# Two feed-forward down projections computed from seven products of halves instead of eight, in a fused three-block kernel on one Trainium2 core

## The chip, the cores and the metric

The kernel runs on one core of one Trainium2 chip. The metric is the device time of one execution in microseconds (us). A change is compared by running the kernel before and the changed one on the same chip.

## The reference

Two layers of a residual block, then a second block of another kind, on 512 tokens of width 1024 in float32. Each of the two layers is a mixer, a cross attention over 256 memory rows and a gated feed-forward, and each of the three is followed by a layer norm over a scaled residual. The change touches the feed-forward:

```
def conv_ffn(x, w_up, conv_w, conv_b, w_down):
    up = x @ w_up                         # 1024 -> 2 * 2816
    a, g = up[..., :D_FF], up[..., D_FF:]
    g = causal_dwconv(g, conv_w) + conv_b
    return (jax.nn.gelu(g) * a) @ w_down  # 2816 -> 1024
x = layer_norm(alpha * x + conv_ffn(...), ln_ffn_g[layer], ln_ffn_b[layer])
```

## The kernel before, in words

Every large product runs in three passes of float32r. An operand is split into a high half (ACT's copy to float32r) and a low half (the operand minus its high half, by DVE), and `mm3` adds high x high, high x low and low x high into one PSUM bank. A matmul has a 128x128 stationary operand and up to 512 moving columns.

Each engine has a program written out by hand; they meet on semaphores only. Weights come in chunks of 128x1024 values (256 rows by 512 columns). `load_to` (SP's queue) fills a ring of NR = 4 RAW buffers, `hi_to` (ACT) makes WH, `lo_to` (DVE) makes WL, both in rings of NH = 5. A chunk's RAW buffer is free when its low half is made; its WH and WL are free when PE has used them (`("used", i)`). So SP loads up to nine chunks ahead of PE, and ACT and DVE split up to five ahead.

The up projection of layer l is eleven column blocks `nb` of four chunks. A block yields two 128-row tiles of `a` and two of `g`, transposed (feature by token), in four PSUM banks. ACT copies g out (L1206), DVE convolves it (L1237 to L1242), ACT applies gelu (L1208), and DVE multiplies with `a` out of PSUM into `hT` (L1245), which holds 22 tiles of 128x512. In layer 1, DVE and SP also stream a vector product (`ada`, L1151 and L1155, with its loads) between the chunks. In layer 0 a value projection (`values_pe`) of the next cross attention stands between up and down.

The down projection (`down_pe`, `down_act`, `down_dve`) is two column halves j of 512. For each there are eleven chunks, with four token tiles t and two row tiles each: 22 x 4 x 3 = 264 matmuls of 512 columns a half, 528 a layer. The activation tile `hT[:, kt, :]` is split by `h_hi` (L1276) and `h_lo` (L1285) into eight slots of XH and XL (the first four of layer 1 into MH and ML). The last four chunks of the second half run token tile by token tile, so that the row norms (L690 to L677 on DVE, L682 and L684 on POOL) begin while PE still multiplies. After layer 0, the rows are transposed for the next stage; after layer 1, ACT squares and scales them (`square_act`, `xn_act`) for the second block.

POOL does little: row statistics (`norm_pool`), the loads of the gains (`load_gb`, L640 and L641) and a few loads for the second block (`early_pool`, L1379 to L1384).

## Time and profile before

| what | value |
|---|---|
| time, median of 3 runs | 1790.11 us (1788.22 to 1790.62) |
| span of the profiled execution | 1786.9 us |
| PE busy | 1761.0 us (99%) |
| DVE busy | 1012.8 us (57%) |
| ACT busy | 648.0 us (36%) |
| POOL busy | 99.3 us (6%) |
| HBM traffic | 181.58 MB read, 6.30 MB written, 105 GB/s |

The profiled execution gives a span and no time of its own beside it; the median of the runs is 3.2 us above that span. A matmul's record in the profile (some 370 to 390 ns) overlaps the next one's, so the number that counts is the distance between two starts.

### The profile page before, as it was taken

The numbers are of one execution on the slowest core, as the hardware profiler recorded it, in microseconds if no ns is written. First come the engines' busy times: TensorE is split into PE (matmuls) and PEld (weight loads), VectorE is DVE, ScalarE is ACT, GpSimd is POOL, SyncE is SP. The second block draws the span as 40 slices with busy tenths as digits, with TensorE's granted clock in tenths as the row PEclk, the third lists the DMA queues.
The fourth block names the chain that finished last, engine by engine and source line by source line (L and its number), as shares of the span: only waits on it lengthen the run. The fifth ranks groups of instructions, "written<-read, shape, count | busy, mean of one in ns | idle before, by whom it ended". The sixth has DMA issues, their size and how long they took to land.

```text
span 1786.9 us, 27394 instructions
## 1 busy us (share of the span) xinstructions
PE 1761.0 (99%) x11539; PEld 1464.1 (82%) x11539; DVE 1012.8 (57%) x1456; ACT 648.0 (36%) x1005; POOL 99.3 (6%) x136
## 2 busy tenths in 40 slices
PE   8999999999999999999999999999999999999998
PEld 7888978988888889888997888888888767777766
DVE  5477256444445555454724755566555585566784
ACT  5232352332234433223234233332433653344552
POOL 3102001000000001000200200000001100011000
PEclk9999999999999999999999999999999999999999
DMA  9323312533333323333331264444331422112512
GB/s 298 114 94 113 112 32 82 158 95 95 96 104 107 94 83 119 112 100 108 117 107 49 75 218 154 142 153 130 125 97 45 151 60 72 38 38 62 176 36 83
DMA packets 146010, 189.67 MB, mean 106 GB/s; under 512 B 7800, under 2 KB 95092, under 8 KB 145120
## 3 DMA queue, kind: packets, MB, share of 16 engines
q1 hardware_dynamic: 140928, 172.59, 31.3%
q0 software_dynamic: 3488, 10.07, 1.8%
q10 hardware_dynamic: 1472, 5.26, 0.8%
q8 instruction: 92, 1.51, 0.4%
q14 instruction: 30, 0.25, 0.0%
HBM read 181.58 MB, written 6.30 MB: 105 GB/s over the span
## 4 chain that ended last, share of the span: by engine, by line
PE 93%; DVE 4%; issue 1%; ACT 1%; POOL 1%; DMA 0%; SPq 0%; DVEq 0%; ACTq 0%
PE ps L326 27%; PE ps L328 27%; PE ps L327 27%; PE ps L965 2%; PE ps L989 2%; PE ps L515 1%; PE ps L2186 1%; PE ps L2206 1%; PE ps L1592 1%; PE ps L2200 1%; PE ps L2220 0%; DVE LATE L2267 0%; PE ps L2323 0%; DVE WL L310 0%; DMA BIG<-mem 0%
## 5 line engine op out<-in xcount | busy, mean ns | idle before, releaser
L310 DVE TENSOR_TENSOR WL<-RAW,WH 128x1024 fp32r<-128x1024 f32 x289 | 350.4, 1222 | 499.6 <-ACT WH L300 498.5
L326 PE MATMUL ps<-XH,WH 128*128 128x512 f32 (+1 forms) x1416 | 523.9, 370 | 3.9 <-DVE XL L1462 2.1
L300 ACT ACTIVATE WH<-RAW 128x1024 fp32r<-128x1024 f32 x289 | 303.4, 1058 | 595.2 <-PE ps L328 569.1
L328 PE MATMUL ps<-XH,WL 128*128 128x512 f32 (+1 forms) x1416 | 517.6, 366 | 0.0
L327 PE MATMUL ps<-XL,WH 128*128 128x512 f32 (+1 forms) x1416 | 517.3, 365 | 0.0
L326 PE MATMUL ps<-WH,XH 128*128 128x512 f32 x784 | 313.5, 400 | 2.4 <-DVE WL L310 1.1
L326 PEld LDWEIGHTS ps<-XH,WH 128*128 128x128 f32 x1416 | 267.1, 189 | 51.7 <-issue 6.6
L328 PE MATMUL ps<-WH,XL 128*128 128x512 f32 x784 | 305.8, 390 | 0.0
L327 PE MATMUL ps<-WL,XH 128*128 128x512 f32 x784 | 305.4, 390 | 0.0
L328 PEld LDWEIGHTS ps<-XH,WL 128*128 128x128 f32 x1416 | 267.1, 189 | 43.5
L327 PEld LDWEIGHTS ps<-XL,WH 128*128 128x128 f32 x1416 | 267.2, 189 | 40.7
L326 PEld LDWEIGHTS ps<-WH,XH 128*128 128x128 f32 x784 | 147.2, 188 | 36.5 <-issue 5.1
L328 PEld LDWEIGHTS ps<-WH,XL 128*128 128x128 f32 x784 | 147.1, 188 | 31.4
L327 PEld LDWEIGHTS ps<-WL,XH 128*128 128x128 f32 x784 | 147.3, 188 | 29.4 <-issue 1.2
L682 POOL TENSOR_SCALAR SM<-SM 128x1 f32<-128x1 f32 x28 | 34.3, 1226 | 1014.0 <-DVE SM L668 1013.7
L1208 ACT ACTIVATE SCR<-SCR,VEC 128x512 f32<-128x512 f32 x44 | 31.8, 724 | 112.6 <-DVE SCR L1242 112.6
L522 ACT ACTIVATE XH<-ps 128x512 fp32r<-128x512 f32 x48 | 25.8, 597 | 107.1 <-PE ps L515 107.0
L1285 DVE TENSOR_TENSOR XL<-BIG,XH 128x512 fp32r<-128x512 f32 x84 | 53.7, 684 | 1.4 <-ACT XH L1276 1.4
L1245 DVE TENSOR_TENSOR BIG<-SCR,ps 128x512 f32<-128x512 f32 x44 | 30.2, 687 | 34.8 <-ACT SCR L1208 34.8
L1276 ACT ACTIVATE XH<-BIG 128x512 fp32r<-128x512 f32 x84 | 47.4, 616 | 2.3 <-PE ps L328 2.3
L326 PE MATMUL ps<-WH,MH 128*128 128x256 f32 (+1 forms) x144 | 42.6, 296 | 0.0
L327 PE MATMUL ps<-WL,MH 128*128 128x256 f32 (+1 forms) x144 | 42.4, 295 | 0.0
(349 smaller groups left out, 1757.3 us busy)
## 6 DMA issues: line engine op xcount, KB each, us to landing
RAW<-ffn_w_up SPq DMA_DIRECT2D x176, 256.0 KB, 3.3
RAW<-ffn_w_down SPq DMA_DIRECT2D x44, 512.0 KB, 3.6
RAW<-w_in SPq DMA_DIRECT2D x33, 512.0 KB, 4.0
RAW<-xa_wkv SPq DMA_DIRECT2D x32, 512.0 KB, 3.9
RAW<-c_w_in SPq DMA_DIRECT2D x24, 512.0 KB, 3.8
LATE<-w_ada SPq DMA_DIRECT2D x24, 512.0 KB, 5.1
RAW<-xa_wq SPq DMA_DIRECT2D x16, 512.0 KB, 5.7
RAW<-xa_wo SPq DMA_DIRECT2D x16, 512.0 KB, 3.7
```

What stands on the lines that cost most here:

```text
L300: e.activation(halves_of(i)[0][:, :, 0:w], raw(i)[:, :, 0:w], ACT.Copy).then_inc(*w_hi.up(i))
L310: e.tensor_tensor(wl[:, :, 0:w], raw(i)[:, :, 0:w], wh[:, :, 0:w].bitcast(F), ALU.subtract).then_inc(*w_lo.up(i))
L326: e.matmul(o, lh, rh, start=start, stop=False)
L327: e.matmul(o, lh, rl, start=False, stop=False)
L328: return e.matmul(o, ll, rh, start=False, stop=stop)
L682: e.tensor_scalar(vr[:, t:t + 1], mv[:, t, 1:2], 1e-5, None, ALU.add).then_inc(*ln_g.up((n, t, "eps")))
L965: r = e.matmul(b[:, 256 * (t % 2):256 * (t % 2) + 256], qT[:, 2 * h + k, 128 * t:128 * t + 128], KT[:, 2 * h + k, :], start=k == 0, stop=k ...
L989: r = e.matmul(b[:, :], VT[:, mt, 256 * h + 128 * d:256 * h + 128 * d + 128], PT[h % 2][:, mt, :], start=mt == 0, stop=mt == 1)
L1208: e.activation(gc[i], gc[i], ACT.Gelu_apprx_tanh, bias=vec(f"fcb{l}", j)).then_inc(*ffn_a.up(("gelu", l, j)))
L1245: e.tensor_tensor(hT[:, j, :], c, ps.tile((("up", l, nb), i))[:, :], ALU.mult).then_inc(*ps.empties((("up", l, nb), i), ffn_v, ("h", l, j)))
L1276: e.activation(h_home(l, j, kt)[0], hT[:, kt, :], ACT.Copy).then_inc(*x_hi.up(("h", l, j, kt)))
L1285: e.tensor_tensor(lo, hT[:, kt, :], hi.bitcast(F), ALU.subtract).then_inc(*x_lo.up(("h", l, j, kt)))
```

## The change

With the activations A (512 x 2816) and the weights B (2816 x 1024) both cut in two along both sides, B11 = rows 0 to 1407 and columns 0 to 511, and so on. Token tiles t are 0 and 1 in the upper half of A, 2 and 3 in the lower one. The four blocks of the output come from

```
S1 = A21 + A22   S2 = S1 - A11   S3 = A11 - A21   S4 = A12 - S2
T1 = B12 - B11   T2 = B22 - T1   T3 = B22 - B12   T4 = B21 - T2
P1 = A11 B11   P2 = A12 B21   P3 = S4 B22   P4 = A22 T4
P5 = S1 T1     P6 = S2 T2     P7 = S3 T3
C11 = P1+P2   C12 = P1+P6+P5+P3   C21 = P1+P6+P7+P4   C22 = P1+P6+P7+P5
```

- **Products.** Seven of 256 x 1408 x 512, each two token tiles by eleven row tiles by three passes: 66 matmuls, 462 a layer. A chunk is now 128 rows of two weight halves (a: B11 and T1; b: T2 and T3; c: B21 and B22) or two row tiles of T4 (e), 39 chunks a layer for 22; each serves 12 matmuls instead of 24 (6 for the last).
- **Weight sums.** `sums_pool` makes T1 to T4 on POOL in the up projection, in 22 steps a layer (row tile k, column half h): two loads of 256 KB with 1 KB pieces, four `tensor_tensor` of 128x256, and one store of 512 KB to HBM (`weight_sums`). Two tiles alternate; the load of step j+1 is issued behind the store of step j and waits for the store of step j-1. SP's loads of the chunks a, b and e wait for the store of their k.
- **Activation sums and items.** `down_pool` makes S1 to S4 by four `tensor_tensor` of 128x256 for each k. The operands of the products are 40 items a layer of 128x512, in order: pairs A (A11 and S1), pairs B (S3 and S2), then C (A12) and D (S4) by turns, then E (A22). ACT makes each item's high half (`item_hi`, L1368 of the changed kernel); DVE makes the low half of A, C and E, and POOL that of B and D (`item_lo_pool`, L1382). Eight slots of XH and XL, as before, with MH and ML for the first four items of layer 1.
- **Order at the end of up.** In layer 1 `item_hi` of items 0 and 1 stands ahead of column block 9, and waits for the last stores of the sums; the two that stood at blocks 4 and 7 are gone. `up_act` and `up_dve` take gelu, convolution and items by turns in block 10.
- **Assembly.** After P1 and P5 (step 20) and P6 and P7 (step 21), ACT copies P1 to SBUF (U), DVE runs twelve operations of 128x512 on U and the rows, and POOL later adds U to six row halves. P2 and P3 end together, then P4 runs by token tile; rows 0 and 1 need P2 and P3, rows 2 and 3 need P4. `early_pool` now stands behind `down_pool`.

```diff
+    FAST = [(name, q + i) for q in range(0, 11, 2) for name in "ab" for i in range(min(2, 11 - q))]
+    FAST += [("c", k) for k in range(11)] + [("e", q) for q in range(6)]
+    def pair(q):
+        return min(2, 11 - 2 * q)
+    def w_fast(l):
+        first["ffn", l] = len(chunks)
+        w = I["ffn_w_down"][l]
+        for name, k in FAST:
+            if name == "a":
+                chunks.append(([((0, 1), 512, w[128 * k:128 * k + 128, 0:512].unsqueeze(1)),
+                                ((1, 2), 512, d_sum[l][k][:, 1:2, :])], 512, (l, k)))
+            if name == "b":
+                chunks.append(([((0, 1), 512, d_sum[l][k][:, 0:1, :]), ((1, 2), 512, d_sum[l][k][:, 3:4, :])], 512, (l, k)))
+            if name == "c":
+                chunks.append(([((0, 2), 512, w[1408 + 128 * k:1536 + 128 * k, :].rearrange("p (k n) -> p k n", k=2))],
+                               512, None))
+            if name == "e":
+                v = d_sum[l][2 * k:2 * k + pair(k)]
+                chunks.append(([((0, pair(k)), 512, v[:, :, 2, :].rearrange("k p n -> p k n"))], 512, (l, 2 * k + pair(k) - 1)))
...
+            if chunks[i][2] is not None:
+                for h in range(2):
+                    e.wait_ge(*sum_out[h].at(chunks[i][2]))
...
+        for nb in range(10):
+            if (l, nb) == (1, 9):
+                item_hi(e, 1, 0)
+                item_hi(e, 1, 1)
             hi_to(e, first["up", l, nb] + 4 + NH)
...
+        hi_to(e, first["up", l, 10] + 3 + NH)
+        for i in range(2):
+            gate_act(e, l, 10, i)
+            item_hi(e, l, i if l == 0 else 2 + i)
+        hi_to(e, first["up", l, 10] + 4 + NH)
+        gelu_act(e, l, 10, 0)
+        if l == 0:
+            item_hi(e, 0, 2)
+        gelu_act(e, l, 10, 1)
+        if l == 0:
+            item_hi(e, 0, 3)
...
+    def item_hi(e, l, n):
+        name, k = ITEMS[n]
+        if l and n < 4:
+            for h in range(2):
+                e.wait_ge(*sum_out[h].at((1, 10)))
+        elif n < 8 + 4 * l:
+            e.wait_ge(*gemm.at((("up", l, 10), 3)))
+        else:
+            e.wait_ge(*gemm.at(("used", first["ffn", l] + item_last(n - 8))))
+        if name in "AB":
+            e.wait_ge(*dn_g.at(("s", l, k)))
+        elif name == "D":
+            e.wait_ge(*dn_g.at(("s4", l, 2 * k + pair(k) - 1)))
+        else:
+            e.wait_ge(*ffn_v.at(("h", l, 10 + 2 * k + pair(k))))
+        e.activation(item_view(n, item_home(l, n)[0]), item_from(n), ACT.Copy).then_inc(*x_hi.up(("item", l, n)))
...
+    def item_lo_pool(e, l, n):
+        e.wait_ge(*x_hi.at(("item", l, n)))
+        hi, lo = item_home(l, n)
+        e.tensor_tensor(item_view(n, lo), item_from(n), item_view(n, hi).bitcast(F), ALU.subtract).then_inc(
+            *x_lo_g.up(("item", l, n)))
...
+    def sum_load(e, l, j):
+        k, h = j // 2, j % 2
+        if k:
+            e.wait_ge(*sum_out[h].at((l, k - 1)))
+        else:
+            e.wait_ge(*(gemm.at(("kvv", 1, 3, 1)) if l else xa_pe.at(("pv", 0, 3, 1))))
+        w = I["ffn_w_down"][l].rearrange("(i r) (j n) -> r i j n", i=2, j=2)
+        to = sum_tile(l, h).rearrange("p (i j n) -> p i j n", i=2, j=2)
+        for i in range(2):
+            e.dma_start(to[:, i, :, :], w[128 * k:128 * k + 128, i, :, 256 * h:256 * h + 256]).then_inc(*sum_in[h].up((l, k)))
+    def sums_pool(e, l):
+        sum_load(e, l, 0)
+        sum_load(e, l, 1)
+        for j in range(22):
+            k, h = j // 2, j % 2
+            x = sum_tile(l, h)
+            b11, b12, b21, b22 = [x[:, 256 * i:256 * i + 256] for i in range(4)]
+            e.wait_ge(*sum_in[h].at((l, k)))
+            e.tensor_tensor(b22, b22, b12, ALU.subtract).then_inc(*sum_g.up(("t3", l, j)))
+            e.tensor_tensor(b12, b12, b11, ALU.subtract).then_inc(*sum_g.up(("t1", l, j)))
+            e.wait_ge(*sum_g.at(("t3", l, j)))
+            e.tensor_tensor(b11, b11, b22, ALU.add).then_inc(*sum_g.up(("t2", l, j)))
+            e.wait_ge(*sum_g.at(("t2", l, j)))
+            e.tensor_tensor(b21, b21, b11, ALU.subtract).then_inc(*sum_g.up(("t4", l, j)))
+            e.wait_ge(*sum_g.at(("t4", l, j)))
+            e.dma_start(d_sum[l][k][:, :, 256 * h:256 * h + 256], x.rearrange("p (i n) -> p i n", i=4)).then_inc(
+                *sum_out[h].up((l, k)))
+            if 1 <= j < 21:
+                sum_load(e, l, j + 1)
+    def down_pool(e, l):
+        if l == 0:
+            e.wait_ge(*rel_out.at("rel"))
+        def rest(k):
+            n = ITEMS.index(("B", k))
+            item_lo_pool(e, l, n)
+            e.wait_ge(*(x_lo.at(("item", l, ITEMS.index(("A", k))))))
+            e.tensor_tensor(hT[:, k, 0:256], hT[:, 11 + k, 0:256], ring[k % 2][:, 256:512], ALU.subtract).then_inc(
+                *dn_g.up(("s4", l, k)))
+        for k in range(11):
+            a11, a21, a22 = hT[:, k, 0:256], hT[:, k, 256:512], hT[:, 11 + k, 256:512]
+            s3, s2 = ring[k % 2][:, 0:256], ring[k % 2][:, 256:512]
+            e.wait_ge(*ffn_v.at(("h", l, 11 + k)))
+            if k >= 2:
+                e.wait_ge(*dn_g.at(("s4", l, k - 2)))
+            e.tensor_tensor(s3, a11, a21, ALU.subtract).then_inc(*dn_g.up(("s3", l, k)))
+            e.wait_ge(*dn_g.at(("s3", l, k)))
+            e.tensor_tensor(a21, a21, a22, ALU.add).then_inc(*dn_g.up(("s1", l, k)))
+            e.wait_ge(*dn_g.at(("s1", l, k)))
+            e.tensor_tensor(s2, a21, a11, ALU.subtract).then_inc(*dn_g.up(("s", l, k)))
+            if k:
+                rest(k - 1)
+        rest(10)
+        for q in range(3):
+            item_lo_pool(e, l, 23 + 2 * q)
+        for u in range(2):
+            e.wait_ge(*ln_v.at((("ffn", l), "sum", u)))
+            for name, t, j in (("x12", u, 1), ("x21", 2 + u, 0), ("x22", 2 + u, 1)):
+                x = XR[:, t, 512 * j:512 * j + 512]
+                e.wait_ge(*ln_v.at((("ffn", l), "p7" if name == "x22" else name, u)))
+                e.tensor_tensor(x, x, U[u], ALU.add).then_inc(*dn_g.up((name, l, u)))
+        for q in range(3, 6):
+            item_lo_pool(e, l, 23 + 2 * q)
...
+        for s, (name, k) in enumerate(ITEMS[0:22]):
+            e.wait_ge(*w_lo.at(i0 + s))
+            ready(s)
+            of = ((1, 0), (5, 256)) if name == "A" else ((6, 256), (7, 0))
+            for half, (p, at) in enumerate(of):
...
+                if name == "ffn":
+                    sums_pool(e, l)
+                    down_pool(e, l)
```

In these rows of program order, names are those of the diff: LAST is POOL's pair of sum tiles, `weight_sums` the sums in HBM, BIG holds `hT`. First POOL in layer 1, from the load of the gains on, before:

```order
L640 DMA GB<-ln_ffn_g 128x1024
L641 DMA GB<-ln_ffn_b 128x1024
L1379 DMA LAST<-w_2 64x512
L1380 DMA LAST<-a_2 64x512
L1382 DMA LAST<-rel_padded 128x8x256
L1384 DMA SCR<-cstd 128x128
```

and in the changed kernel, from behind the same two loads on:

```order
L1398 DMA LAST<-ffn_w_down 128x2x256 x4
L1409 TENSOR_TENSOR LAST<-LAST 128x256
L1410 TENSOR_TENSOR LAST<-LAST 128x256
L1412 TENSOR_TENSOR LAST<-LAST 128x256
L1414 TENSOR_TENSOR LAST<-LAST 128x256
L1416 DMA weight_sums<-LAST 512x1x256
L1409 TENSOR_TENSOR LAST<-LAST 128x256
L1410 TENSOR_TENSOR LAST<-LAST 128x256
L1412 TENSOR_TENSOR LAST<-LAST 128x256
L1414 TENSOR_TENSOR LAST<-LAST 128x256
L1416 DMA weight_sums<-LAST 512x1x256
L1398 DMA LAST<-ffn_w_down 128x2x256 x2
```

The loads that stood right behind the gains come after 22 such steps and the whole of `down_pool`. Next POOL at the start of the first changed down projection (L1437 to L1441 are S3, S1 and S2, L1382 the low half of a B item, L1429 is S4):

```order
L1437 TENSOR_TENSOR BIG<-BIG 128x256
L1439 TENSOR_TENSOR BIG<-BIG 128x256
L1441 TENSOR_TENSOR BIG<-BIG 128x256
L1382 TENSOR_TENSOR XL<-BIG,XH 128x512
L1429 TENSOR_TENSOR BIG<-BIG 128x256
L1437 TENSOR_TENSOR BIG<-BIG 128x256
L1439 TENSOR_TENSOR BIG<-BIG 128x256
L1441 TENSOR_TENSOR BIG<-BIG 128x256
```

The last five of these rows are what POOL repeats for each k; before, POOL had nothing in this place. Last, ACT in layer 1 in the changed kernel (L1254 copies g out, L1259 is gelu, L327 the weights' high halves, L1368 an item's), from the end of column block 8:

```order
L1254 ACTIVATE SCR<-ps 128x512
L1259 ACTIVATE SCR<-SCR,VEC 128x512
L1368 ACTIVATE MH<-BIG 128x512 x2
L327 ACTIVATE WH<-RAW 128x1024 x4
L1254 ACTIVATE SCR<-ps 128x512
L1259 ACTIVATE SCR<-SCR,VEC 128x512
L1254 ACTIVATE SCR<-ps 128x512
L1259 ACTIVATE SCR<-SCR,VEC 128x512
L327 ACTIVATE WH<-RAW 128x1024 x3
L1254 ACTIVATE SCR<-ps 128x512
```

The two items stand ahead of all of ACT's work for block 9; before, the row L300 x4 followed gelu at once.

## Rows read from the trace of the kernel before

**Rows 1.** The page: busy time of each engine, and PE's clock in slices.

```profile
PE 1761.0 (99%) x11539; PEld 1464.1 (82%) x11539; DVE 1012.8 (57%) x1456; ACT 648.0 (36%) x1005; POOL 99.3 (6%) x136
...
PEclk9999999999999999999999999999999999999999
```

**Rows 2.** Windows, second down projection, PE (span, busy, count, clock, DMA, GB/s).

```profile
1265.30:1384.90 119.60, 119.60 (x529) 1.00 0.28 87
```

**Rows 3.** Timeline of DVE, first down projection (start us, us, what, [idle before]).

```profile
603.05 1.23 DVE L310 TENSOR_TENSOR WL<-RAW,WH 128x1024 fp32r<-128x1024 f32 x1 [3.01 <-ACT WH L300]
604.19 1.28 DVE L1285 TENSOR_TENSOR XL<-BIG,XH 128x512 fp32r<-128x512 f32 x2
```

**Rows 4.** Timeline of ACT, same place and columns.

```profile
601.96 1.06 ACT L300 ACTIVATE WH<-RAW 128x1024 fp32r<-128x1024 f32 x1 [3.34 <-PE ps L328]
602.92 1.14 ACT L1276 ACTIVATE XH<-BIG 128x512 fp32r<-128x512 f32 x2
```

**Rows 5.** Windows of the two up projections, all engines (busy us, count).

```profile
313.00:552.00 239.00, 239.00 (x1143) 201.63 (x1142) 110.51 (x133) 72.37 (x88) 0.43 (x1) 1.00 0.36 108
1026.00:1265.00 239.00, 239.00 (x1142) 201.31 (x1142) 141.33 (x188) 73.04 (x90) 0.38 (x1) 1.00 0.50 157
```

**Rows 6.** The page: DMA issues of the whole run.

```profile
RAW<-ffn_w_up SPq DMA_DIRECT2D x176, 256.0 KB, 3.3
RAW<-ffn_w_down SPq DMA_DIRECT2D x44, 512.0 KB, 3.6
```

**Rows 7.** POOL, grouped by line and form (xcount | busy us, mean ns | idle before).

```profile
L1550 POOL TENSOR_TENSOR LAST<-LAST,SM 128x512 f32<-128x512 f32 x4 | 4.0, 1040 | 13.1 <-DVE SM L1534 13.1
...
L1373 POOL TENSOR_SCALAR SM<-SM 128x1 f32<-128x1 f32 x4 | 0.8, 190 | 10.7 <-ACT SCR L1365 10.7
```

**Rows 8.** Timeline of POOL at a row norm of the last down projection.

```profile
1370.56 1.31 POOL L682 TENSOR_SCALAR SM<-SM 128x1 f32<-128x1 f32 x1 [91.43 <-DVE SM L668]
...
1375.19 0.19 POOL L1373 TENSOR_SCALAR SM<-SM 128x1 f32<-128x1 f32 x1 [2.67 <-ACT SCR L1365]
```

**Rows 9.** Timeline of DVE at the same place.

```profile
1370.51 1.28 DVE L671 SCALAR_TENSOR_TENSOR XR<-XR,SM,GB 128x1024 f32<-128x1024 f32 x1
```

**Rows 10.** Timeline of POOL before the first up projection's gains are loaded.

```profile
309.20 1.40 POOL L684 TENSOR_TENSOR SM<-SM 128x1 f32<-128x1 f32 x1
...
312.91 0.53 POOL L641 DMA_DIRECT2D GB<-ln_ffn_b  x1
```

**Rows 11.** Timeline of DVE at the same place.

```profile
308.95 1.22 DVE L310 TENSOR_TENSOR WL<-RAW,WH 128x1024 fp32r<-128x1024 f32 x1
```

**Rows 12.** DMA issues from 1020 to 1040 us (KB each, us to landing).

```profile
GB<-ln_ffn_g POOLq DMA_DIRECT2D x1, 512.0 KB, 4.2
GB<-ln_ffn_b POOLq DMA_DIRECT2D x1, 512.0 KB, 5.9
```

**Rows 13.** DMA issues, whole run, the largest load on POOL's queue.

```profile
LAST<-rel_padded POOLq DMA_DIRECT2D x1, 1024.0 KB, 7.4
```

**Rows 14.** Timeline of POOL where the second up projection's gains are loaded.

```profile
1025.85 0.53 POOL L641 DMA_DIRECT2D GB<-ln_ffn_b  x1
```

**Rows 15.** Timeline of ACT in the last two column blocks of the second up projection.

```profile
1220.10 1.06 ACT L300 ACTIVATE WH<-RAW 128x1024 fp32r<-128x1024 f32 x1 [4.38 <-PE ps L328]
...
1228.51 1.04 ACT L300 ACTIVATE WH<-RAW 128x1024 fp32r<-128x1024 f32 x1
...
1242.81 1.06 ACT L300 ACTIVATE WH<-RAW 128x1024 fp32r<-128x1024 f32 x1 [4.38 <-PE ps L328]
```

**Rows 16.** Timeline of ACT at the end of the first up projection.

```profile
552.64 1.06 ACT L300 ACTIVATE WH<-RAW 128x1024 fp32r<-128x1024 f32 x1 [4.38 <-PE ps L328]
```

**Rows 17.** Timeline of DVE, the last row norm of the second down projection.

```profile
1385.13 0.69 DVE L690 SCALAR_TENSOR_TENSOR XR<-XR,ps 128x512 f32<-128x512 f32 x1 [0.34 <-PE ps L328]
```

More of the change, by code:

```diff
@@ L1278, in h_lo @@
[L1278 to L1292 removed]
+            if (l, nb) == (1, 9):
+                item_lo(e, 1, 0)
+                item_lo(e, 1, 1)
@@ new lines, in up_dve @@
+            for c in range(4 if nb else 0):
+                if l:
+                    side()
+                lo_to(e, first["up", l, nb] + min(c + 1, 3 if nb == 10 else 4) + NH)
+                if l:
+                    side()
+            if nb < 10:
+                lo_to(e, first["up", l, nb] + 4 + NH)
+                for i in range(2):
+                    conv_dve(e, l, nb, i)
+                    gated_dve(e, l, nb, i)
+        conv_dve(e, l, 10, 0)
+        if l == 0:
+            item_lo(e, 0, 0)
@@ L1297, in behind @@
                 turn_pe(e, n, t)
-        if l == 0:
-            values_pe(e, 1, 0)
-        for j in range(2):
-            gemm_n(e, (*n, j), lambda kt, t, j=j: h_x(l, j, kt, t), 11, final=behind if j else None, ready=lambda kt, j=j: x_lo.at(("h", l, j, kt)))
+        for u in range(2):
+            ps.take(("down", l, 4, u))
+            for w in ps.vacant(("down", l, 4, u)):
+                e.wait_ge(*w)
+        for q in range(2):
+            for u in range(2):
+                last(q, u)
@@ L1303, in down_act @@
+        for u in range(2):
+            for q in range(2, 6):
+                last(q, u)
+                if (u, q) in ((0, 5), (1, 3)):
+                    behind(u)
+        ps.back(*[("down", l, 4, u) for u in range(2)])
     def down_act(e, l):
-        n = ("ffn", l)
+        n, i0 = ("ffn", l), first["ffn", l]
+        limit = n_in2 if l else n_chunks
+        item_hi(e, l, 4)
         if l == 0:
             values_act(e, 1, 0)
-        for c in range(11):
-            hi_to(e, first[(*n, 0)] + c + 1 + NH)
-            h_hi(e, l, 0, c + 3)
```

371 lines of the change are left out of this document (250 added, 121 removed).

## Prediction

> **What bounds the kernel now.** The page comes first: PE is busy for 99% of the span, and its granted clock is the higher of its two levels (2.4 GHz) in every slice, while DVE, ACT and POOL have room [rows 1]. So the down projections cost what PE's matmuls cost, and the window over the second one shows it: PE is busy in all of its 119.60 us, with 529 matmuls started, which is 0.2265 us each [rows 2]. Inside it DVE works 2.4 us and ACT 2.1 us for each chunk of 5.44 us [rows 3, 4]. Nothing in this stage is waited for but PE. The two up projections are as full [rows 5], so all that the change adds there lies beside PE, if it keeps its due times.
>
> **What is removed.** 66 matmuls a layer, 132 in all: 132 x 0.2265 = 29.9 us from the path of PE. The form of the matmuls and their operands' sizes are the same, so I take the same distance between starts.
>
> **What is added on ACT and DVE.** A chunk or an item now serves 12 matmuls, 2.72 us. DVE needs 1.14 us for a weight low half (the distance of its start to the next) and 0.64 for an item [rows 3], so for a pair k of an A and a B item (5.44 us of PE) 2 x 1.14 + 0.64 = 2.9 us. ACT needs 2 x 1.06 + 2 x 0.57 = 3.3 us [rows 4]. Both fit; cost nothing while PE is the cover. A chunk every 2.72 us asks 193 GB/s of SP's queue. Loads of 512 KB land 3.6 us after their issue, and those in two pieces of 256 KB after 3.3 each [rows 6]; a RAW buffer comes round every 4 x 2.72 = 10.9 us and needs about 3.7 + 1.1 + 1.2 = 6 of them. No cost.
>
> **POOL in the down projection.** Here the cover is thinnest. A POOL `tensor_tensor` of 128x512 took 1.04 us, a 128x1 operation 0.19 [rows 7]; I put 128x256 between them, at 0.62. For each k POOL runs four of these and one of 512: 3.5 us, some 4.0 with gaps of 0.09. Alone it would keep up with 5.44. But a POOL operation waits for DVE: the 128x1 operation that takes 0.19 us where DVE is not at work took 1.31 where DVE had just begun 1.28 us on two SBUF operands [rows 8, 9], and a second one 1.40 where the next DVE operation of that kind ran [rows 10, 11]. All of DVE's weight and item low halves have two SBUF operands. If the two engines excluded each other in full, a k would take 3.5 + 2.9 = 6.4 us; if POOL fills DVE's pauses well, 5.44 or less. The waits of the trace are all of POOL for DVE, and part of POOL's time (the 0.19) moves no data, so I take 6.0. The due times: item A3 is needed 5 x 2.72 = 13.6 us after A0, and POOL makes its two k by 2 x 6.0 = 12.0, ACT and DVE add 1.2, which leaves 0.4. From A3 to A9 PE takes 12 items, 32.6 us, and POOL six k, 36.0. That is 3.4 - 0.4 = 3.0 us of waiting a layer, 6.0 for both. At 5.44 it is nothing, at 6.4 it is 6.2 a layer, 12.4 for both; these are the ends.
>
> The Trainium skill (SBUF — State Buffer, Who interferes with whom) says that a DVE instruction with two SBUF inputs and a GpSimd instruction that reads SBUF exclude each other, whichever began first. The trace agrees for POOL behind DVE, at 1.31 us for 0.19; no row shows DVE behind POOL. By that rule the sum would have the 12.4 us in place of 6.0.
>
> **The weight sums in the up projection.** One step is four additions, a store and, behind it, the two loads of the next step, whose landing it then waits for. The additions take 4 x 0.62 + 0.3 = 2.8 us alone; DVE is busy for 59% of the second up projection [rows 5] and can hold each of them up by 0.35, which gives 4.2; I take 3.4. The DMA part: two loads of 512 KB on POOL's queue, issued 0.62 us apart, landed 4.2 and 5.9 us after their own issues [rows 12], so the second ended 2.3 us behind the first, and what is fixed is 1.9. A load of 1024 KB with 1 KB pieces took 7.4 [rows 13]. If the store and the loads share the queue one behind the other, landing is 1.9 + 2.3 + 2.3 = 6.5 us after the store's issue; if they run side by side, 1.5 of issuing, 1.9 and 1.2 make 4.6. I take the middle, 5.6. Of the 22 steps 20 wait so: 22 x 3.4 + 20 x 5.6 + 1.6 for two bare stores = 188 us, between 155 and 224.
>
> The room in layer 1: the last load of the gains is issued at 1025.85 [rows 14], lands 5.9 later, and the first sums' rows some 2.3 after that, at 1034. ACT now stands at item 0 of block 9, where before it split weights at 1228.51; it has the high half of block 10's first chunk since 1220.10, and block 10 begins at 1242.8, when the chunk before it is used [rows 15]. So PE runs until 1242.8 + 5.4 = 1248.2, and ACT must be back by 1246.0. From the last store's issue to there go S of k 0 and 1 and the item, 5.7 us. That leaves 1240.3 - 1034 = 206 us. 188 fits, 224 is 18 us late. In layer 0 nothing is needed before PE has left up (552.6 [rows 16]) and the value projection behind it (5.5 us more): from 312.91 [rows 10] + 8.2 to 553.7 are 232 us, which holds even 224. So this costs nothing at what I take, 18 us at its upper end. What is covered here has no cover beyond 18 us of slack; that is the step with the largest error.
>
> **The ends of the stage.** P3 takes the banks of P5, due 4.1 and 4.8 us after item 20 ends; DVE frees them after six operations of 0.65, at 3.9, if ACT's copies are there: 0.3 us a layer, from 0 to 2. Rows 0 and 1 now start together, when P2 and P3 are done, and DVE needs about 7.5 us each (with four adds and statistics of 0.7, two passes of 1.28, POOL's 0.85 and a weight of 1.14); PE comes to the transposes of row 1 after 24 + 21 + 12 matmuls and the first transposes, at 13.8: 1.0 us in layer 0. Row 3 of layer 1 used to begin 0.2 us behind PE's last matmul [rows 17], with its rows 5.44 us apart and 0.34 of it idle; P4's tiles come 4.76 apart: 0.35 us. `early_pool` moves behind `down_pool`, which ends when item 33 is split, about 35 us before the stage's end; its largest load takes 7.4 us [rows 13]: nothing.
>
> **Sum.** -29.9 + 6.0 + 0.6 + 1.0 + 0.35 = -22 us. It is made against the span of 1786.9, which the median of the runs exceeds by 3.2; taken off the median of 1790.1 it gives **1768 us**.
>
> **Rivals.**
> - *All hidden.* POOL slips between DVE's operations. For it: DVE waits 3.0 us in each chunk [rows 3], and POOL alone needs 4.0 of 5.44. Against it: the waits of [rows 8 to 11]. Only the 2 us at the ends stay: 1790.1 - 29.9 + 2 = 1762, from 1759 to 1764.
> - *DVE and POOL exclude each other in full*, the 6.4 us a k: 1790.1 - 29.9 + 12.4 + 2 = 1775, up to 1779 if the burst of twelve DVE operations comes on top. This is the rule named above. For it: POOL's waits; against it: no DVE operation in the trace is longer for POOL's sake.
> - *The sums come late in layer 1 only*, by up to 18 us: PE stands still in block 10 for just as long: 1774 to 1786. For it: up is also where DMA is busiest, 157 GB/s without the sums in layer 1 [rows 5].
> - *The sums come late in both layers*, and the kernel is slower than before. It decides from 24 us of lateness on, which is 230 us for the 22 steps. If the sums' DMAs take 7.5 us a step beside the other streams, the steps take 22 x 4.2 + 20 x 7.5 + 1.6 = 244 us, 38 late in layer 1 and 12 in layer 0, and 9 from the rest: 1790.1 - 29.9 + 59 = 1819. Against it: the load that was longest for its size took 7.4 us for twice the loads' bytes.
> - *The gain isn't made*: the matmuls go but start further apart, because two of the halves and the weights change every 12 matmuls. Nothing in the window of [rows 2] depends on the chunk, so this has little: about 1790.
>
> **Chances.** The forecast's own case (1764 to 1774) has 0.45, all hidden 0.23, full exclusion 0.12, late in layer 1 0.11, late in both 0.06, no gain 0.03. A measurement of this kernel tells 0.2%, 3.6 us, from no change. Faster by more: the first four, less a little of the late case, 0.90; within it 0.04; slower 0.06. The range 1759 to 1785 leaves out the last two cases, the end of the late one and a tail below.
>
> **What would show it.** In the profile of the changed kernel: 132 matmuls fewer, still 0.2265 us apart; in the A and B part of both down projections pauses of PE behind POOL's item low halves, 2 to 4 us in each; POOL operations of 128x256 between 0.6 and 1.9 us, the long ones beside DVE; a sum step of some 9 us; the last store of the sums in layer 1 before 1240 and no pause of PE in block 10. Wrong would be: a pause of PE of more than 3 us in block 10 of layer 1 (the sums), DVE operations stretched beyond 1.3 us (exclusion both ways), or a PE pause at P3's or P4's first matmul (banks).

## The result

The changed kernel took 1856.1 us, the median of four runs (1854.62 to 1859.96), against 1790.4 us before: a ratio of 1.0374, with a 95% interval from 1.0362 to 1.0387. It is 3.7% slower; the prediction was faster by 1.2%. The profiled execution spans 1854.8 us.

From the page of the changed kernel: busy time of each engine, the granted clock in 40 slices, the chain that ended last, and the three groups of DMAs that are new.

```profile
PE 1756.0 (95%) x11407; PEld 1451.7 (78%) x11407; DVE 1110.9 (60%) x1468; ACT 677.9 (37%) x1035; POOL 528.8 (29%) x578
...
PEclk9999999999999999999999999996999899999999
...
PE 50%; POOL 20%; DMA 13%; DVE 11%; issue 4%; ACT 2%; SPq 0%; ACTq 0%; DVEq 0%; POOLq 0%
...
RAW<-weight_sums SPq DMA_DIRECT2D x68, 256.0 KB, 3.6
...
LATE<-ffn_w_down POOLq DMA_DIRECT2D x44, 256.0 KB, 4.6
weight_sums<-LATE POOLq DMA_DIRECT2D x22, 512.0 KB, 3.4
```

The 132 matmuls are gone (11539 in [rows 1]), but PE's busy time fell by only 5 us, and it is now 99 us short of the span, where it was 26 short. The clock falls in two slices, and 44% of the chain that ended last is POOL, DMA and DVE, where before they had 5% of it.

The time splits at the starts of five matmuls that both kernels have: the first of each down projection, the first 128x512 one of the stage behind the first down projection, the first one behind the last product of the second down projection (it makes a bias tile), and the first product of the second block. In us, each with what it would be if only the matmuls had gone:

| stretch | before | bare gain | changed |
|---|---|---|---|
| down projection of layer 0 and the rows' turn behind it | 152.8 | 137.8 | 167.8 |
| from there to the down projection of layer 1, up projection included | 554.4 | 554.4 | 587.4 |
| down projection of layer 1 | 119.7 | 104.7 | 133.4 |
| from the end of its products to the second block's first | 11.5 | 11.5 | 17.0 |
| all the rest | 948.6 | 948.6 | 949.3 |

So 30.0, 33.0, 28.6 and 5.5 us were lost at four places. The two down projections lose for the same reasons, the stretch between them for another. First the largest single pause: PE stood still in block 10 of layer 1's up projection. These are PE's own rows at the places of its longest pauses (start us, us, engine, line, operation, and in brackets the idle time before it with its releaser). Where the text counts pauses, it takes the distance of two starts less 0.2265 us, which is some 0.15 more than the idle time in brackets:

```profile
570.64 0.80 PE L359 MATMUL ps<-WH,XH 128*128 128x512 f32 x1 [5.02 <-DVE WL L337]
...
638.95 0.77 PE L359 MATMUL ps<-WH,XH 128*128 128x512 f32 x1 [4.83 <-DVE XR L1581]
...
1290.61 0.80 PE L359 MATMUL ps<-XH,WH 128*128 128x512 f32 x1 [29.63 <-DVE SM L1195]
...
1394.41 0.77 PE L359 MATMUL ps<-WH,XH 128*128 128x512 f32 x1 [4.71 <-DVE XR L1581]
...
1438.55 0.50 PE L359 MATMUL ps<-WH,XH 128*128 128x512 f32 x1 [3.66 <-DVE WL L337]
```

The releaser of the 29.6 us is a small DVE operation of the side work, which is only the last link. ACT's own rows at that time show the first:

```profile
1285.24 0.63 ACT L1368 ACTIVATE MH<-BIG 128x512 fp32r<-128x512 f32 x1 [42.45 <-DMA weight_sums<-LAST]
1287.65 0.63 ACT L1368 ACTIVATE MH<-BIG 128x512 fp32r<-128x512 f32 x1 [1.79 <-POOL BIG L1441]
1288.19 3.88 ACT L327 ACTIVATE WH<-RAW 128x1024 fp32r<-128x1024 f32 x4
```

ACT stood 42.5 us at item 0 of the second down projection, whose home is `MH`, until the last store of the weight sums had landed. Four high halves of weights were queued behind it, DVE had nothing to split, and PE ran dry. POOL's rows of the last steps of those sums show how long one takes:

```profile
1272.84 0.75 POOL L1416 DMA_DIRECT2D weight_sums<-LAST  x1 [0.30 <-POOL LAST L1414]
1273.51 1.42 POOL L1398 DMA_DIRECT2D LAST<-ffn_w_down  x2
1278.63 0.71 POOL L1409 TENSOR_TENSOR LAST<-LAST 128x256 f32<-128x256 f32 x1 [3.70 <-DMA LAST<-ffn_w_down]
1279.32 0.71 POOL L1410 TENSOR_TENSOR LAST<-LAST 128x256 f32<-128x256 f32 x1
1280.00 0.71 POOL L1412 TENSOR_TENSOR LAST<-LAST 128x256 f32<-128x256 f32 x1
1280.79 0.72 POOL L1414 TENSOR_TENSOR LAST<-LAST 128x256 f32<-128x256 f32 x1
1281.81 0.75 POOL L1416 DMA_DIRECT2D weight_sums<-LAST  x1 [0.30 <-POOL LAST L1414]
```

This step, with DVE idle, took 9.0 us. Over all of layer 1 the first addition began at 1049.8 and the last store at 1281.8: 232 us, 11.0 a step; in layer 0 it was 322.0 to 546.3, 10.7 a step. The waits of the whole run, grouped by who waits for whom (us in total, times, longest), say how much of it is the loads:

```profile
POOL LAST L1409 <- DMA LAST<-ffn_w_down: 103.5, 21, 7.6
...
POOL LATE L1409 <- DMA LATE<-ffn_w_down: 93.6, 21, 6.6
ACT XH L1368 <- POOL BIG L1441: 72.8, 18, 4.6
...
PE ps L359 <- DVE WL L337: 28.9, 16, 5.0
```

The loads are 4.9 us of waiting a step in layer 1 (103.5 / 21), and 2.1 of issuing lie ahead of them.

The first and the third line of the table are the down projections. There POOL's rows over two k of the A and B part of layer 1 read:

```profile
1339.67 1.80 POOL L1382 TENSOR_TENSOR XL<-BIG,XH 128x512 fp32r<-128x512 f32 x1 [2.27 <-ACT XH L1368]
1341.43 1.71 POOL L1429 TENSOR_TENSOR BIG<-BIG 128x256 f32<-128x256 f32 x1
1343.29 1.53 POOL L1437 TENSOR_TENSOR BIG<-BIG 128x256 f32<-128x256 f32 x1
1344.89 0.74 POOL L1439 TENSOR_TENSOR BIG<-BIG 128x256 f32<-128x256 f32 x1
1345.71 0.74 POOL L1441 TENSOR_TENSOR BIG<-BIG 128x256 f32<-128x256 f32 x1
1346.41 1.30 POOL L1382 TENSOR_TENSOR XL<-BIG,XH 128x512 fp32r<-128x512 f32 x1
...
1354.44 1.80 POOL L1382 TENSOR_TENSOR XL<-BIG,XH 128x512 fp32r<-128x512 f32 x1 [2.27 <-ACT XH L1368]
```

and DVE's in the same stretch:

```profile
1340.57 3.66 DVE L337 TENSOR_TENSOR WL<-RAW,WH 128x1024 fp32r<-128x1024 f32 x2 [0.24 <-ACT WH L327]
1347.21 1.04 DVE L1376 TENSOR_TENSOR XL<-BIG,XH 128x512 fp32r<-128x512 f32 x1 [2.99 <-ACT XH L1368]
1348.18 1.76 DVE L337 TENSOR_TENSOR WL<-RAW,WH 128x1024 fp32r<-128x1024 f32 x1
1352.93 0.69 DVE L1376 TENSOR_TENSOR XL<-BIG,XH 128x512 fp32r<-128x512 f32 x1 [2.99 <-ACT XH L1368]
1353.87 1.23 DVE L337 TENSOR_TENSOR WL<-RAW,WH 128x1024 fp32r<-128x1024 f32 x1 [0.25 <-ACT WH L327]
```

POOL's sums take 0.74 us alone and 1.53 or 1.71 beside DVE, its low half 1.30 or 1.80; and DVE's weight low half takes 1.23 alone, as in [rows 3], but 1.76 or more beside POOL. POOL comes round in 14.77 us for two k, 7.4 a k against PE's 5.44: 6.25 of work, stretched, and 1.1 of waiting for ACT, which splits the second of two A items and a weight before the B item that POOL waits for. PE paused eight times in this part of layer 1, for 12.7 us together. Last, the windows over the pauses (busy us of each engine, granted clock as a share of 2.4 GHz, DMA share, GB/s):

```profile
570.00:575.00 5.00, 4.36 (x10) 3.48 (x11) 5.00 (x4) 2.47 (x4) 4.70 (x4) 0.50 0.55 160
...
1262.00:1290.00 28.00, 0.00 (x0) 0.00 (x0) 2.48 (x3) 2.98 (x4) 16.48 (x23) 0.57 0.29 94
1290.00:1295.00 5.00, 4.39 (x10) 3.48 (x11) 4.90 (x8) 2.56 (x4) 0.00 (x0) 0.50 0.63 173
1295.00:1300.00 5.00, 5.00 (x20) 4.07 (x19) 4.14 (x7) 1.21 (x2) 0.00 (x0) 0.84 0.75 242
```

After the pause of 5.0 us and after the one of 29.6 PE worked at 0.50, the lower level (1.2 GHz): 10 matmuls in 4.4 us, where at 0.2265 us each it would be 19. So a pause costs more than its own length: 33.0 us for the one of 29.8.

### The profile page after: what moved, and what is told of

The parts are those of the page before. It is cut to its first block, busy times and chain, and to the rows that moved or that the text cites. A ratio compares the mean times of both kernels' runs of the same rounds, so it can differ in the third digit from the quotient of the medians.

```text
span 1854.8 us, 27838 instructions
## 1 busy us (share of the span) xinstructions
PE 1756.0 (95%) x11407; PEld 1451.7 (78%) x11407; DVE 1110.9 (60%) x1468; ACT 677.9 (37%) x1035; POOL 528.8 (29%) x578
## 4 chain that ended last, share of the span: by engine, by line
PE 50%; POOL 20%; DMA 13%; DVE 11%; issue 4%; ACT 2%; SPq 0%; ACTq 0%; DVEq 0%; POOLq 0%
PE ps L359 14%; PE ps L360 13%; PE ps L361 13%; DMA LAST<-ffn_w_down 6%; DMA LATE<-ffn_w_down 6%; DVE WL L337 3%; POOL weight_sums L1416 2%; POOL BIG L1437 2%; PE ps L1001 1%; PE ps L1025 1%; POOL LATE L1409 1%; POOL BIG L1429 1%; POOL XL L1382 1%; POOL LAST L1414 1%; POOL LATE L1410 1%
## 5 line engine op out<-in xcount | busy, mean ns | idle before, releaser
L337 DVE TENSOR_TENSOR WL<-RAW,WH 128x1024 fp32r<-128x1024 f32 x323 | 425.3, 1331 | 382.3 <-ACT WH L327 381.1
L359 PE MATMUL ps<-XH,WH 128*128 128x512 f32 (+1 forms) x1416 | 526.9, 372 | 36.1 <-DVE SM L1195 29.6
L327 ACT ACTIVATE WH<-RAW 128x1024 fp32r<-128x1024 f32 x323 | 338.1, 1056 | 504.5 <-PE ps L361 452.8
L359 PE MATMUL ps<-WH,XH 128*128 128x512 f32 x740 | 303.3, 410 | 37.8 <-DVE WL L337 27.4
L361 PE MATMUL ps<-WH,XL 128*128 128x512 f32 x740 | 292.8, 396 | 0.0
L360 PE MATMUL ps<-WL,XH 128*128 128x512 f32 x740 | 292.4, 395 | 0.0
L361 PEld LDWEIGHTS ps<-WH,XL 128*128 128x128 f32 x740 | 141.2, 191 | 31.1
L1259 ACT ACTIVATE SCR<-SCR,VEC 128x512 f32<-128x512 f32 x44 | 31.9, 724 | 127.6 <-DVE SCR L1303 127.6
L1368 ACT ACTIVATE XH<-BIG 128x512 fp32r<-128x512 f32 (+1 forms) x76 | 45.5, 602 | 73.6 <-POOL BIG L1441 72.8
L1376 DVE TENSOR_TENSOR XL<-BIG,XH 128x512 fp32r<-128x512 f32 (+1 forms) x44 | 38.8, 882 | 49.2 <-ACT XH L1368 49.2
L1382 POOL TENSOR_TENSOR XL<-BIG,XH 128x512 fp32r<-128x512 f32 (+1 forms) x32 | 52.0, 1630 | 28.8 <-ACT XH L1368 28.7
L1409 POOL TENSOR_TENSOR LATE<-LATE 128x256 f32<-128x256 f32 x22 | 27.2, 1235 | 93.6 <-DMA LATE<-ffn_w_down 93.6
```

Source lines behind the costliest of these rows:

```text
L327: e.activation(halves_of(i)[0][:, :, 0:w], raw(i)[:, :, 0:w], ACT.Copy).then_inc(*w_hi.up(i))
L337: e.tensor_tensor(wl[:, :, 0:w], raw(i)[:, :, 0:w], wh[:, :, 0:w].bitcast(F), ALU.subtract).then_inc(*w_lo.up(i))
L359: e.matmul(o, lh, rh, start=start, stop=False)
L360: e.matmul(o, lh, rl, start=False, stop=False)
L361: return e.matmul(o, ll, rh, start=False, stop=stop)
L1368: e.activation(item_view(n, item_home(l, n)[0]), item_from(n), ACT.Copy).then_inc(*x_hi.up(("item", l, n)))
```

## The experiments

The theory that came out of these rows has **two causes**: the sums of weights come late (33 us), and POOL and DVE hold one another up in the down projections (most of 58 us). The rival for each was that the loss would stay when its alleged cause went: that the added DMA traffic or the added work itself is what costs. What a later run changes is told against the changed kernel unless it says otherwise.

**1. The loads earlier.** In each step the next step's two loads are issued behind the third addition, not behind the store.

```
+            if 1 <= j < 21:
+                sum_load(e, l, j + 1)      # behind t2, ahead of the fourth addition
...
-            if 1 <= j < 21:
-                sum_load(e, l, j + 1)      # behind the store
```

> The loads of the next sums step are issued behind the third addition instead of behind the store. Theory (the sums are late because each step waits for a load that is issued last): a step falls from 10.5 us to about 8.2, the last store of layer 1 is issued near 1230 us instead of 1281.8, and the 29.8 us pause of PE in column block 10 of layer 1 is gone, with the low clock behind it: 33 us less, about 1822 us. The pauses inside both down projections stay (20 and 21 us). Rival (the step is bound by the DMA engines, which also carry weights and the ada stream): a step of 10 us or more, and a pause still above 20 us, 1845 us or more.

It took 1821.5 us (1.0172 of before, 1.0143 to 1.0202), 34.6 less. The step of layer 1 fell to 9.5 us, where 8.2 were hoped for, as POOL now waits for the store before it can load into the tile behind it:

```profile
1235.76 1.72 POOL L1412 TENSOR_TENSOR LAST<-LAST 128x256 f32<-128x256 f32 x1
1238.69 1.45 POOL L1398 DMA_DIRECT2D LAST<-ffn_w_down  x2 [1.21 <-DMA weight_sums<-LAST]
1240.16 0.75 POOL L1416 TENSOR_TENSOR LAST<-LAST 128x256 f32<-128x256 f32 x1
1241.20 0.75 POOL L1418 DMA_DIRECT2D weight_sums<-LAST  x1 [0.30 <-POOL LAST L1416]
```

But the last store went out at 1247.2 in place of 1281.8, and that is enough: the pause in block 10 is gone, the stretch between the down projections takes 554.4 us, that of before, and no other stretch changed by more than 1.1. The same bytes move in both, so it was not their amount that cost the 33 us but when the last of them landed.

**2. The items of layer 1 later.** The high and low halves of items 0 to 3 of layer 1 stand where layer 0 has them, in block 10, so that ACT and DVE split block 10's weights before they wait for item 0.

```
-            if (l, nb) == (1, 9):
-                item_hi(e, 1, 0)
-                item_hi(e, 1, 1)
...
-            item_hi(e, l, i if l == 0 else 2 + i)
+            item_hi(e, l, i)
```

> The sums are untouched; only the high and low halves of items 0 to 3 of layer 1 are moved from the top of column block 9 to behind the copies of block 10, as in layer 0. Theory (PE stands still because ACT is parked at item 0 with all its weight work behind it, not because PE needs the item): ACT goes on, the last store still comes near 1282 us, PE ends block 10 near 1280 and waits for the first item until about 1288; the pause falls from 29.8 us to 6 to 10, total about 1833 us. Rival (the sums' lateness is paid in full wherever the wait stands): no change, 1855 us.

It took 1836.8 us (a single run), 19.3 less. PE runs block 10 and stops at the first item instead:

```profile
1291.78 0.77 PE L359 MATMUL ps<-WH,MH 128*128 128x512 f32 x1 [13.78 <-issue]
```

So 30 us of pause became 14, and the stretch between the down projections lost 13.9 us in place of 33.0: less than half of the price was the lateness itself, the rest was what the program order had put behind the wait. The pause came out 4 to 8 us longer than expected; the last store was issued at 1286.5 in this run, not near 1282.

**3. DVE's part of the collision smaller.** The low halves of the weights in the a and b chunks are made for half their columns only; the other half of `WL` keeps old values, so this run leaves that part of the correction out.

```
+            if any(first["ffn", l] <= i < first["ffn", l] + 22 for l in range(2)):
+                w = 256
```

> DVE makes the low halves of the A and B chunks for 256 of each 512 columns only; the rest of WL keeps old values. So DVE's two-operand work for a k falls from 2.9 us to about 1.8, and POOL's is untouched. Theory (DVE and POOL exclude each other, so that a k costs the sum of their times, 7.38 us now): about 6.2 us a k, PE's pauses in the A and B part fall from 12 to about 5 us a layer, the bank pause of 5 us at P3 too, total about 1836 us. Rival (POOL is too slow by itself, or its chain of waits is): POOL's period stays 7.38 us a k, total 1853 to 1856.

It took 1832.0 us (a single run), 24.1 less. POOL's item low halves begin 12.74 us apart for two k, 6.4 a k in place of 7.4, with the wait for ACT still in it:

```profile
1324.13 1.29 POOL L1384 TENSOR_TENSOR XL<-BIG,XH 128x512 fp32r<-128x512 f32 x1 [2.27 <-ACT XH L1370]
...
1336.86 1.29 POOL L1384 TENSOR_TENSOR XL<-BIG,XH 128x512 fp32r<-128x512 f32 x1 [2.27 <-ACT XH L1370]
```

Nothing of POOL's own work was taken away. A shorter DVE operation made POOL faster, which is the collision and not POOL's load.

**4. POOL's part smaller.** The four sums of a k are made for 16 of 256 columns from k = 2 on (the rest keep old values).

```
+            m = 256 if k < 2 else 16
+            a11, a21, a22 = hT[:, k, 0:m], hT[:, k, 256:256 + m], hT[:, 11 + k, 256:256 + m]
```

> POOL's S1 to S4 are made for 16 columns of 256 (from k = 2 on), so most of the activation sums are left out; all waits and the order stay. Theory (the time of POOL's additions beside DVE makes the pauses): POOL needs some 2.5 us a k, the pauses of the A and B part (12 and 13 us) and the 5 us at P3's bank in each layer go to 0 to 2 us, total about 1822 us; the pause in block 10 of layer 1 stays. Rival (the chain item B behind item A through ACT and POOL binds, 2.27 us of waiting in each two k): pauses of at least 5 us a layer stay, total 1840 us or more.

It took 1813.0 us (a single run), 43.1 less. Of the pauses in the A and B parts one of 1.3 us is left, and the ones at P3's bank fell from about 5 us to 0 and 1.1: they were DVE's lateness, carried on. The two down stretches took 146.3 and 114.9 us. This is what the down projections cost if the sums of hidden rows were nearly free, and layer 1 is still 10 us above its bare 104.7; 5.2 of them are the pause at the last e chunk, 1.1 the one at P3's bank.

**5. The same work on DVE.** S1 to S4 and the low halves of the B and D items (not of weights, as the expectation has it) move to DVE, POOL keeps the additions of U. The sums of weights stay as the change has them.

```
-    on_pool = ("B", "D")
+    on_pool = ()
...
+            rest_dve(e, l, s + 7)          # S4 of this k, S3, S1, S2 of k + 2
```

> All of S1 to S4 and the low halves of the B and D weights move from POOL to DVE; POOL keeps only the additions of U at the down projection's end. The weight sums in the up projection stay as in the change. Theory 'POOL and DVE hold each other up in the down projection': without POOL there, DVE has 4.9 us of work a k at its undisturbed durations (L337 at 1.22, two items' low halves, four sums of about 0.35 each) against 5.44 us of PE, so the pauses of 1.3 to 2.3 us in the A/B part and most of the 5 us at P3's bank go in both layers, about 34 us with the clock behind them as in the run with narrow sums; the pause of about 29 us in block 10 of layer 1 stays: about 1,820 us. Rival 'what takes the time is the work itself, wherever it runs': DVE becomes the engine that is waited for, pauses of 0.5 to 1.5 us stay at each k, and the time is 1,835 us or more.

It took 1822.7 us (a single run), 33.4 less, with 122 operations more on DVE and as many fewer on POOL. In the down projections one of these sums takes 0.42 or 0.43 us there against 0.73 to 1.72 on POOL. The down stretches are 152.7 and 115.8 us. That DVE itself becomes the bound is true only at the start of each stage (5.1 us in layer 0, and 1.2 and 0.8 in layer 1), where five items come at once. At the end, the pause of 4.9 us at layer 1's last e chunk is still there.

**6. Both.** Runs 1 and 5 together.

> Both edits together: the loads of the next step's two blocks issued behind the third of the step's four additions instead of behind its store, and the sums of the down projection on DVE. Theory 'two separate causes, one in each projection': the first alone gave 1,821.5 us (34.6 below the change), the second should give about as much, and since they act at different places they add up: 1,785 to 1,790 us, the time of the kernel before, with the pauses at P3's bank, at the last e chunk and in the tail left. Rival 'the two hide one another' (the late sums also set the start of the down items): 1,800 us or more.

It took 1787.4 us (1785.8 to 1791.9, eight runs; 0.9990 of before, 0.9979 to 1.0001). The two gains, 34.6 and 33.4, made 68.7 together, so the causes are separate, and with them undone the change costs nothing. Nor does it gain anything clear of noise: 29.9 us of matmuls are gone and the time is that of before. From its page:

```profile
PE 1741.0 (98%) x11407; PEld 1444.5 (81%) x11407; DVE 1147.5 (64%) x1590; ACT 679.1 (38%) x1035; POOL 376.4 (21%) x456
...
PE 83%; DVE 12%; issue 2%; DMA 1%; ACT 1%; POOL 1%; SPq 0%; DVEq 0%; ACTq 0%
```

Layer 0's stretch is 149.6 and layer 1's 116.6, each 3 us better than before and not 15; the one behind layer 1 is 16.5 where 11.5 was. At P3's bank no pause is left in either layer. The rest of the study asked where these 29 us are.

**7. The order at the stage's end, first try.** To run 6: the last e chunk's low half inside row 0's work, and P5 taken out of its bank before the two x11 rows.

```
             row(t)
+            if t < 1:
+                lo_to(e, min(i0 + 34 + NH, limit))
```

> As the run with both edits, and two changes of order on DVE: the low half of the last e chunk's weight item stands in front of the second row instead of behind the first row's whole work, and the evacuation of P5 stands ahead of the two x11 rows, so that the bank for P3 comes free earlier. Theory: each of the pauses of 3.8 to 4.9 us at these places was DVE's order and nothing else, so 3 to 4 of them (both layers) go and the time falls by 6 to 12 us against the run with both edits alone: 1,775 to 1,782 us, below the kernel before. Rival 'the pauses at the end are the latency of P3's own chain': the pause only moves to the next bank, and the time is within 2 us of the run with both edits alone.

It took 1787.6 us (0.9988 of before, 0.9977 to 1.0000): no gain. In layer 1 the pause of 4.95 us at the last e chunk became one of 2.7 there and one of 2.8 at the transposes behind it. The time is the rival's, but its reason is not shown: P3's bank had cost nothing in run 6, so that half of the edit had nothing to gain.

**8. The rows in another order.** To run 6: the last e chunk's low half ahead of row 0, row 1's first addition between row 0's norm and its end, POOL's square root of the next row ahead of the RMS scale.

```
+        lo_to(e, min(i0 + 34 + NH, limit))
+        first_half(0); second_half(0); norm(0)
+        first_half(1); row_end(0); second_half(1); norm(1)
```

> As the run with both edits (1,787.4 us), and the rows' work on DVE at the down projections' end put in another order: the low half of the last e chunk stands ahead of row 0 instead of behind it, row 1's first addition and statistics stand between row 0's norm and its end (where DVE waited 0.83 to 0.85 us for POOL's square root), and in layer 1 POOL makes the next row's square root before the row's own RMS scale. Theory 'these pauses are DVE's order': the pause of 4.95 us before the last e chunk in layer 1 goes with the 2 to 3 us of half clock behind it, the tail of layer 1 shortens from 13.1 us by about 4, in layer 0 the pauses of 0.9 and 1.9 us go: 10 to 14 us less, 1,773 to 1,778 us, under the kernel before. Rival 'the earlier work only moves the pause', as when the low half was put inside row 0 and P5's evacuation first (1,787.6): 1,784 us or more.

It took 1787.2 us (0.9989 of before, 0.9980 to 0.9999). Layer 1's down projection fell from 116.6 to 109.1 us, as expected, and the stretch behind it rose from 16.5 to 23.5, where the theory had it fall; the whole lies in the rival's range. ACT's rows there show why: row 3 left DVE at 1383.7, but its square stands at 1387.07, behind row 2's scale, bias copies and a weight.

```profile
1384.11 1.15 ACT L1694 ACTIVATE BIG<-XR,SM 128x1024 f32<-128x1024 f32 x1 [1.87 <-POOL SM L1700]
1385.17 1.06 ACT L1760 ACTIVATE VH<-ps 128x512 f32<-128x512 f32 x2
1386.12 1.06 ACT L328 ACTIVATE WH<-RAW 128x1024 fp32r<-128x1024 f32 x1
1387.07 1.05 ACT L1690 ACTIVATE SCR<-XR 128x1024 f32<-128x1024 f32 x1
```

**9. The start spread out.** To run 8: a weight item between the items at each down projection's start, and in layer 1 two items and their sums in block 10.

```
+            if m == 5:
+                lo_to(e, i0 + 1 + NH)
```

> As the run before it, and the start of the down projection spread out: one weight item's halves stand between the second and third item of hidden rows instead of behind all five, and in layer 1 the low halves of the first two B items, with the sums behind them, are made in block 10. Theory: DVE's queue of five items and twelve sums is what PE waits for at the start, 3.3 us in layer 0 and 1.35, 1.2 and 0.8 us in layer 1, with about 1.5 us of half clock behind the first: 4 to 7 us less than the run before it. Rival 'DVE has no slack at the start, the order only moves the wait from the weight item to the item of hidden rows': within 1.5 us of the run before it.

It took 1784.9 us (0.9974 of before, 0.9964 to 0.9983). That is 2.3 less than run 8, between the 4 to 7 of the theory and the rival's 1.5, and the two intervals overlap. The profiles can't settle it, since the execution profiled took 1785.5 us in run 8, the least of its ten, and 1788.5 here, the most of ten. In them the pause of 3.3 us in layer 0 fell to 1.1 and 0.7, and new ones of 1.1 and 1.6 stand at P3's bank and at layer 1's first items. Undecided.

**10. The chain of rows shortened.** To run 8: ACT squares row 3 before the copies and the weight, row 3's addition stands ahead of row 2's end on DVE, and in layer 0 the transposes of rows 0 and 1 stand later among PE's products.

```
-                if (u, q) in ((0, 5), (1, 3)):
-                    behind(u)
+                if (u, q) in ((1, 3), (1, 5)):
+                    behind(q // 4)
```

> As the run with the rows reordered (1,787.2 us), whose profile shows why it gained nothing: in layer 1 PE finished the down projection at 1,369.7 but waited until 1,393.2 for the second block's first matmul, and row 3, done on DVE at 1,383.7, was squared by ACT only at 1,387.1, behind two copies of bias tiles, a weight item and row 2's scale. Here ACT squares row 3 ahead of those, row 3's addition stands ahead of row 2's end on DVE (two waits for POOL's root of 0.8 us go), and in layer 0 the transposes of rows 0 and 1 stand 2.7 and 1.4 us of products later in PE's order, where pauses of 1.9 and 2.1 us stood. Theory 'the end of the down projection is bound by the chain of rows, DVE to ACT to POOL to ACT to PE, and not by PE': 3 to 4 us less at the tail, 2 to 4 in layer 0: 1,780 to 1,783 us. Rival 'the chain has another link of the same length' (PE's banks or the transposes' own time): 1,785 us or more.

It took 1783.9 us (1780.9 to 1784.1, five runs; 0.9959 of before, 0.9946 to 0.9973), just above the expected range and below the rival's. It is faster than both kernels, than the one before by 0.4%. The stretch behind layer 1 is 20.7 us, layer 0's 146.2.

The stretches of the runs that carry the reading, in us:

| stretch | before | changed | 1 | 5 | 6 | 8 | 10 |
|---|---|---|---|---|---|---|---|
| layer 0, with the turn | 152.8 | 167.8 | 166.7 | 152.7 | 149.6 | 148.4 | 146.2 |
| to layer 1's down projection | 554.4 | 587.4 | 554.4 | 586.4 | 554.6 | 554.4 | 555.0 |
| layer 1's down projection | 119.7 | 133.4 | 133.3 | 115.8 | 116.6 | 109.1 | 109.0 |
| behind it | 11.5 | 17.0 | 17.1 | 16.3 | 16.5 | 23.5 | 20.7 |

The last two lines added are 131.2 before and 129.7 in run 10. Of the 15 us of layer 1, run 10 has 4.3 of loss left inside the down projection, and 9.2 are given back behind the last product. With seven products rows 0 and 1 become complete only when P2 and P3 are, rows 2 and 3 when P4 is, so DVE's norms of four rows, which ran beside products before, come at the end in one chain: in run 10 DVE works on rows from 1361.4 to 1381.4, while PE's last product is over at 1368.7. PE's rows of run 10:

```profile
1373.99 0.55 PE L1754 MATMUL ps<-CST,BIG 128*128 128x128 f32 x3 [1.69 <-ACT BIG L1695]
1375.92 0.55 PE L1754 MATMUL ps<-CST,BIG 128*128 128x128 f32 x3 [1.38 <-DVE XR L1587]
1382.12 5.80 PE L1754 MATMUL ps<-CST,BIG 128*128 128x128 f32 x26 [5.66 <-DVE VH L1766]
```

PE does little but transposes from 1372 to the second block's first product at 1389.4. That this chain is the bound there is read from the rows and supported by the 2.9 us that run 10 took off it; a kernel in which the rows cost nothing was not run.

## Why the prediction was wrong

**The 29.9 us of matmuls**: right. At full clock they still start 0.2265 us apart, and run 4 has 114.9 us in layer 1 with the pauses of the A and B part gone, 4.8 below the kernel before. The rival of no gain from the matmuls fell. Two other terms failed, and all three signs that the prediction named for being wrong came: a pause in block 10, DVE operations beyond 1.3 us, and a pause at P3's first matmul.

**The sums of weights** are the first step that failed: they stood in the sum at nothing, and cost 33.0 us. The prediction took 9.0 us a step (3.4 of additions, 5.6 of DMA), 188 in all, at most 224, and a room of 206. The room was right: the gains' load was issued at 1040.06, 14.2 us later than in [rows 14], and so was the date, 1240.3 + 14.2 - 1049.8 = 205. The 22 steps took 232. The DMA part was 7.0 a step (2.1 of issuing, 4.9 of waiting), above the 6.5 that I had for store and loads one behind the other, and the additions 4.0, near my upper 4.2 (0.71 to 0.74 us each alone, not 0.62: POOL's 1.04 for 128x512 in [rows 7] had one of its operands in `SM`, and with two full tiles it takes 1.30, and up to 1.8 beside DVE). So the sums were 26 us late and PE's pause was 29.8. What had no price at all was the clock behind the pause, 3 us. The text called this the step with the largest error and still gave lateness in layer 1 only 18 us at most. "Late in both layers" did not happen either: layer 0 kept its date with 224 us of the 232.

**POOL in the down projection** is the second: it stood in the sum at 6.0 us for both layers, and run 5, which takes the work off POOL, gave 33.4 back. The work of a k was near: 6.25 us against the 6.0 taken. Two things were missing: the wait for ACT, 1.1 a k, which comes from ACT's order, and that DVE is held up as well. No row of before showed DVE behind POOL; rows of the changed kernel do: 1.23 became 1.76 and more. By the rule of the Trainium skill (SBUF — State Buffer, Who interferes with whom), a DVE instruction with two SBUF inputs and a GpSimd instruction that reads SBUF exclude each other whichever came first; the trace agrees in both directions, 0.74 to 1.53 us on POOL and 1.23 to 1.76 on DVE. The prediction's figure for full exclusion (6.4 a k) was still below the 7.4 that came, since its POOL operations were too short: with 0.73 and 1.30 for 0.62 and 1.04 the same sum is 4 x 0.73 + 1.30 + 2.9 = 7.1. Layer 1 alone had 12.7 us in its eight pauses.

**The ends of the stage**, and its start. P3's bank was priced at 0.3 us a layer, at most 2; it cost 5.0 and 4.9. Run 4 shows that this is not the bank's own chain but the lateness of DVE and POOL arriving there: with the sums narrow it was 0 and 1.1. The last e chunk was not priced at all: 3.8 us, as its low half stood behind all of row 0 on DVE. The turn in layer 0 was 1.0 by the forecast; pauses of 0.9, 1.9 and 2.8 us stood there. The last row was 0.35 from [rows 17]; it was 5.5. It had been reckoned from P4's own spacing, as if DVE were there on time, while rows 0 to 3 were one queue that PE had left behind. The start of layer 0 (5.2 us) was not in the sum; only the rival of full exclusion had up to 4 us for a burst of DVE operations.

**The clock.** Every price was for PE at the higher level. In layers 0 and 1 the pauses add up to 22.4 and 21.4 us of the 30.0 and 28.6 lost; most of the other 7 to 8 us each lie in windows such as that from 570 to 575, where the granted clock was 0.50. Not every pause had this price: from 577 to 637, with four pauses of 1.3 to 2.3 us, it stayed at 1.00.

Undoing the two wrong steps gave the time before and not the forecast of 1768. Run 6 is still 11.8 us above the bare gain in layer 0, 11.9 in layer 1 and 5.0 behind it: the starts and the ends of the stages, with their clock. These could be moved and made shorter (runs 8 to 10) but were not removed. A form of the change that makes the forecast true was not found.

## What to carry to other kernels

When work is added to an idle engine under a deadline, price a step from its longest serial path, store, issue and landing included, and then ask what stands in program order behind the instruction that waits for it: the pause in block 10 was 30 us for work that was some 26 late, and half of it went by moving the instructions that wait. An engine at 6% of the span isn't free by that alone: beside DVE's operations on two SBUF tiles, what POOL did in 0.73 us alone took up to 1.7 and held DVE up by half a microsecond, while DVE itself did it in 0.42. And a form with fewer products that delivers its outputs late and together gives up the overlap of what follows; count the rows behind the last product before counting the products.
